# The first sixteen modulation tiles on TensorE, and the first norm in two groups, in a two-layer diffusion trunk

## The reference

```python
mod = silu(cond) @ ada_w[l] + ada_b[l]      # 9 x 1024 numbers, once for c_ctx and once for c
h   = x * rsqrt(mean(x * x) + 1e-6) * g[0] * (1 + scale) + shift
y   = (silu(h @ w_gate) * (h @ w_up)) @ w_down
```

## Time and profile before

| | |
|---|---|
| median of 3 timed runs | 2817.86 us (2813.22 to 2823.29) |
| the profiled execution | 2814.35 us, span 2812.5 us |
| PE busy | 2671.0 us, 95% |
| DVE busy | 1471.0 us, 52% |
| ACT busy | 1040.7 us, 37% |
| DMA | 320.21 MB, mean 114 GB/s |
| mean granted PE clock | 0.97 |

### The profile page before, as it was taken

One profiled execution on the slowest core, in us unless ns is written; L12 is line 12 of the kernel. 1 busy time (PEld: TensorE's weight loads), 2 busy tenths in 40 slices (PEclk: granted clock), 3 DMA queues, 4 the chain that ended last, 5 costly groups with the idle time before them and its releaser, 6 DMA issues.

```text
span 2812.5 us, 41918 instructions
## 1 busy us (share of the span) xinstructions
PE 2671.0 (95%) x17263; PEld 2556.0 (91%) x17263; DVE 1471.0 (52%) x2362; ACT 1040.7 (37%) x1574; POOL 3.7 (0%) x5
## 2 busy tenths in 40 slices
PE   6999999998886999999999999999989989999998
PEld 6999999885676889999999999999878888999998
DVE  6888334533436367763356775336565436322334
ACT  4333343444543353222345322334433345222333
POOL 0000000000000000000000000000000000000000
PEclk7999999999987999999999999999989999999999
DMA  6666234320000145542445553344210013322344
GB/s 237 209 204 207 77 130 149 123 68 24 1 1 23 53 144 186 185 134 95 149 134 181 188 187 112 108 151 142 73 60 1 1 60 106 112 75 75 105 146 140
DMA packets 87771, 320.21 MB, mean 114 GB/s; under 512 B 12486, under 2 KB 16598, under 8 KB 87126
## 3 DMA queue, kind: packets, MB, share of 16 engines
q1 hardware_dynamic: 87638, 318.37, 34.0%
HBM read 312.44 MB, written 3.23 MB: 112 GB/s over the span
## 4 chain that ended last, share of the span: by engine, by line
PE 87%; DVE 7%; ACT 4%; issue 1%; DMA 1%; SPq 1%; DVEq 0%; ACTq 0%
PE ps L2119 41%; PE ps L2148 30%; PE ps L949 2%; PE ps L707 2%; PE ps L2177 2%; PE ps L567 1%; ACT w_hi L402 1%; DVE w_lo L408 1%; PE ps L512 1%; DVE xsq L1924 1%; PE ps L935 1%; PE ps L938 1%; PE ps L937 1%; DVE hx_lo L1933 1%; PE ps L1323 0%
## 5 line engine op out<-in xcount | busy, mean ns | idle before, releaser
L408 DVE TENSOR_TENSOR w_lo<-w_raw,w_hi 128x1024 fp32r<-128x1024 f32 (+1 forms) x384 | 521.3, 1358 | 943.2 <-ACT w_hi L402 942.5
L402 ACT CAST w_hi<-w_raw 128x1024 fp32r<-128x1024 f32 (+1 forms) x384 | 443.9, 1156 | 1227.9 <-PE ps L2119 715.8
L2119 PE MATMUL ps<-hx_hi,w_hi 128*128 128x320 f32 x2688 | 612.5, 309 | 6.9 <-DVE w_lo L408 3.2
L2119 PE MATMUL ps<-hx_lo,w_hi 128*128 128x320 f32 x2688 | 611.6, 308 | 0.0
L2119 PE MATMUL ps<-hx_hi,w_lo 128*128 128x320 f32 x2688 | 611.3, 308 | 0.0
L2119 PEld LDWEIGHTS ps<-hx_hi,w_hi 128*128 128x128 f32 x2688 | 450.7, 188 | 8.0 <-DVE w_lo L408 3.7
L2119 PEld LDWEIGHTS ps<-hx_hi,w_lo 128*128 128x128 f32 x2688 | 451.1, 188 | 0.0
L2119 PEld LDWEIGHTS ps<-hx_lo,w_hi 128*128 128x128 f32 x2688 | 451.0, 188 | 0.0
L2148 PE MATMUL ps<-hh_hi,w_hi 128*128 128x320 f32 x1408 | 435.5, 309 | 3.0 <-DVE hh_lo L2013 3.0
L2148 PE MATMUL ps<-hh_lo,w_hi 128*128 128x320 f32 x1408 | 433.3, 308 | 0.0
L2148 PE MATMUL ps<-hh_hi,w_lo 128*128 128x320 f32 x1408 | 433.3, 308 | 0.0
(11 more groups left out here) (291 smaller groups left out, 2699.1 us busy)
## 6 DMA issues: line engine op xcount, KB each, us to landing
w_raw<-in_ffn_gu SPq DMA_DIRECT2D x212, 512.0 KB, 3.6
w_raw<-in_ffn_dn SPq DMA_DIRECT2D x128, 704.0 KB, 4.0
ring_a<-in_ada_w SPq DMA_DIRECT2D x96, 512.0 KB, 4.6
ada_top<-in_ada_w SPq DMA_DIRECT2D x32, 512.0 KB, 4.6
w_raw<-in_even_in SPq DMA_DIRECT2D x16, 512.0 KB, 3.6
w_raw<-in_odd_in SPq DMA_DIRECT2D x12, 512.0 KB, 4.4
first_a<-in_ada_w SPq DMA_DIRECT2D x8, 512.0 KB, 12.0
w_raw<-in_even_out SPq DMA_DIRECT2D x8, 512.0 KB, 3.7
```

The costliest lines, as they stand in the source:

```text
L402: nc.scalar.copy(w_hi[:, slot, 0:tiles * P], w_raw[:, slot, 0:tiles * P]).then_inc(hi_done, 1)
L408: nc.vector.tensor_tensor(w_lo[:, slot, 0:tiles * P], w_raw[:, slot, 0:tiles * P], w_hi[:, slot, 0:tiles * P], ALU.subtract).then_inc(lo_d ...
L2119: last = nc.tensor.matmul(ps[:, out_bank + h, 0:TH], w, a[:, k, h * TH:(h + 1) * TH], start=(start and w is wh and a is hi), stop=(stop an ...
```

## The change

All sixteen tiles are made by PE, in the order (0, 8), (1, 9), ..., so that shift and scale of a feature tile come together. They are taken from a new layout `ada_first`, and their sums go into banks 6 (feature tiles 0 to 3) and 7 (4 to 7). DVE finishes the mods of four feature tiles at a time, and makes the norm of these four in both halves (all scaled tiles, then all low parts) before the low part of one weight chunk; then the next four. ACT follows in the same order. `cond_b` is loaded last and its silu is made last; DVE waits for it before block 0. ACT loads the table that has both Ln and Exp once, ahead of the squares. SP loads chunk 0 between the two groups of eight tiles and chunk 1 after the second.

```diff
-        first_order = [0, 1, 8, 2, 3, 9, 4, 5, 10, 6, 7, 11, 14, 12, 15, 13]
-        by_pe, by_dve = range(KT, KT + 6), (*range(KT), 14, 15)
+        first_order = [j for k in range(KT) for j in (k, KT + k)]
+        def nth_in(i, h, k):
+            return nth(i, h, k) if i else KT * (k // 4) + 4 * h + k % 4 + 1
...
-            sp.dma_start(cond_col[:], io["cond_col"]).then_inc(col_loaded, 16)
-            load_cond()
+            for dst, name in ((cond_col, "cond_col"), (ada_bias, "ada_b"), (norm_g, "norm_g")):
+                sp.dma_start(dst[:], io[name]).then_inc(col_loaded, 16)
...
-            for q in range(2):
-                load(q, q, ffn_gu[0, 0, q], 8, wait=False)
+            load_first(range(KT))
+            load(0, 0, ffn_gu[0, 0, 0], 8, wait=False)
+            load_first(range(KT, 2 * KT))
+            load(1, 1, ffn_gu[0, 0, 1], 8, wait=False)
+            sp.dma_start(cond_b[:], io["cond"]).then_inc(cond_loaded, 16)
...
-            silu_cond(0)
+            nc.scalar.preload_act_table_set("natural_log_exp_and_others")
...
-                    for q in range(2):
-                        split_hi(act, q, q, 8, wait_used=False)
-                    high(0, 0, every)
-                    high(0, 1, every)
+                    split_hi(act, 0, 0, 8, wait_used=False)
+                    for g in range(2):
+                        for h in range(2):
+                            high(0, h, range(4 * g, 4 * g + 4))
+                    split_hi(act, 1, 1, 8, wait_used=False)
+                    silu_cond(0)
...
-            dve.wait_ge(cond_ready, 1)
-            for i, j in enumerate(by_dve):
-                wait_first(dve, j)
-                ada_column(ada_first(j), j, first_used, i)
-            dve.wait_ge(first_used, len(by_dve))
-            dve.wait_ge(scale_done, len(by_pe))
-            link(dve, dve_chain, nc.vector.tensor_copy(mods[:, KT:KT + len(by_pe), :],
-                                                       ps[:, 7, 0:2 * len(by_pe)].rearrange("p (j c) -> p j c", c=2)))
-            finished(0, 0, 0, 2).then_inc(mods_ready, 1)
-            dve.wait_ge(mods_ready, 1)
-            for q in range(2):
-                split_lo(dve, q, q, 8, wait_used=False)
+            def first_mods(g):
+                dve.wait_ge(scale_done, g + 1)
+                for part in range(2):
+                    cols = slice(KT * part + 4 * g, KT * part + 4 * g + 4)
+                    ins = nc.vector.tensor_tensor(mods[:, cols, :], ps[:, 6 + g, 8 * part:8 * part + 8].rearrange(
+                        "p (j c) -> p j c", c=2), ada_bias[:, cols].unsqueeze(2).broadcast_to((P, 4, 2)), ALU.add)
+                link(dve, dve_chain, ins)
+                for ci in range(2):
+                    ins = nc.vector.scalar_tensor_tensor(out=mods[:, cols, ci], in0=mods[:, cols, ci], scalar=1.0,
+                                                         in1=norm_g[:, 0, 0, 4 * g:4 * g + 4], op0=ALU.add, op1=ALU.mult)
+                ins.then_inc(mods_ready, 1)
+                dve.wait_ge(mods_ready, g + 1)
...
-                    normed(0, 0)
-                    normed(0, 1)
+                    dve.wait_ge(col_loaded, 48)
+                    for g in range(2):
+                        tiles = range(4 * g, 4 * g + 4)
+                        first_mods(g)
+                        for h in range(2):
+                            scaled(0, h, tiles)
+                        for h in range(2):
+                            low(0, h, tiles)
+                        split_lo(dve, g, g, 8, wait_used=False)
+                    dve.wait_ge(cond_ready, 1)
...
             def first_scales():
                 pe.wait_ge(col_ready, 1)
-                for i, j in enumerate(by_pe):
-                    wait_first(pe, j)
-                    for k in range(KT):
-                        ins = nc.tensor.matmul(ps[:, 7, 2 * i:2 * i + 2], ada_first(j)[:, k * P:(k + 1) * P],
-                                               cond_col[:, k, :], start=(k == 0), stop=(k == KT - 1))
+                for g in range(2):
+                    for i in range(KT * g, KT * g + KT):
+                        j = first_order[i]
+                        a = 8 * (j // KT) + 2 * (j % 4)
+                        wait_first(pe, j)
+                        for k in range(KT):
+                            ins = nc.tensor.matmul(ps[:, 6 + g, a:a + 2], ada_first(j)[:, k * P:(k + 1) * P],
+                                                   cond_col[:, k, :], start=(k == 0), stop=(k == KT - 1))
                     ins.then_inc(scale_done, 1)
```

More of the change, by code:

```diff
@@ L310, in build @@
         ada_loaded = [sem(f"ada_loaded{q}") for q in range(ADA_RING)]
-        first_used, ada_used = sem("first_used"), sem("ada_used")
+        ada_used = sem("ada_used")
         silu_done, mul_done, hhi_done, block_free = sem("silu_done"), sem("mul_done"), sem("hhi_done"), sem("block_free")
@@ L1544, in load_ada, with load_first @@
                 sp.dma_start(ada_ring(n), ada_w[ADA_FIRST + n]).then_inc(ada_loaded[n % ADA_RING], 16)
-            sp.dma_start(cond_col[:], io["cond_col"]).then_inc(col_loaded, 16)
-            load_cond()
+            for dst, name in ((cond_col, "cond_col"), (ada_bias, "ada_b"), (norm_g, "norm_g")):
+                sp.dma_start(dst[:], io[name]).then_inc(col_loaded, 16)
             for k in range(KT):
                 sp.dma_start(xT[:, k, :], io["x"][:, k, :]).then_inc(x_loaded, 16)
-            for i, j in enumerate(first_order):
-                src = io["ada_scale"][j - KT] if j in by_pe else ada_w[j]
-                sp.dma_start(ada_first(j), src).then_inc(first_loaded[i // 4], 16)
+            def load_first(tiles):
+                for i in tiles:
+                    j = first_order[i]
+                    sp.dma_start(ada_first(j), io["ada_first"][j]).then_inc(first_loaded[i // 4], 16)
             def load(c, slot, src, tiles, wait=True):
@@ L1650, in silu_cond @@
             def silu_cond(i):
-                act.wait_ge(cond_loaded, 48 * (i + 1))
+                act.wait_ge(cond_loaded, 16 + 48 * i)
                 nc.scalar.activation(cond_b[:], cond_b[:], ACT.Silu).then_inc(cond_ready, 1)
-            act.wait_ge(col_loaded, 16)
+            act.wait_ge(col_loaded, 48)
             nc.scalar.activation(cond_col[:], cond_col[:], ACT.Silu).then_inc(col_ready, 1)
-            silu_cond(0)
+            nc.scalar.preload_act_table_set("natural_log_exp_and_others")
             def rms(bank, h, sums, value, done):
@@ L1679, in high @@
                 for k in tiles:
-                    act.wait_ge(pre_ready, nth(i, h, k))
+                    act.wait_ge(pre_ready, nth_in(i, h, k))
                     for ci, a, b in half_groups(h):
@@ L1773, in _ @@
                             nc.scalar.copy(causal_b[:, :, i, :], causal[:]).then_inc(attn_const, 1)
-                    act.wait_ge(mods_ready, min(s["f"], 2) + 2)
+                    act.wait_ge(mods_ready, min(s["f"], 2) + 3)
                     nc.scalar.preload_act_table_set("natural_log_exp_and_others")
@@ L1930, in low @@
                 for k in tiles:
-                    dve.wait_ge(hxhi_ready, nth(i, h, k))
+                    dve.wait_ge(hxhi_ready, nth_in(i, h, k))
                     for ci, a, b in half_groups(h):
@@ L2037, in _ @@
                                 ins.then_inc(mods_ready, 1)
-                                dve.wait_ge(mods_ready, s["f"] + 2)
+                                dve.wait_ge(mods_ready, s["f"] + 3)
                     else:
@@ L2144, in half_product @@
                     if ready is not None:
-                        pe.wait_ge(hx_ready, ready + t)
+                        pe.wait_ge(hx_ready, ready(t))
                     wh, wl = w_hi[:, q, t * P:(t + 1) * P], w_lo[:, q, t * P:(t + 1) * P]
@@ L2161, in in_products @@
                         half_product(2 * q + h, q, hx_hi, hx_lo, 0, KT, h, True, True,
-                                     ready=None if q else nth(i, h, 0), count=h == 1)
+                                     ready=None if q else lambda t: nth_in(i, h, t), count=h == 1)
             def post_sums(i, h):
@@ L2214, in gu_half @@
                             half_product(4 * par + 2 * q + h, q, hx_hi, hx_lo, 0, KT, h, True, True,
-                                         ready=nth(n, h, 0) if q == 0 and st in (0, lag) else None)
+                                         ready=(lambda t: nth_in(n, h, t)) if q == 0 and st in (0, lag) else None)
                             if st == 0 and q == 0 and after:
@@ L2294, in lay_out @@
     out["cond_col"] = c(np.stack([f["c_ctx"], f["c"][0]]).T.reshape(KT, P, 2).transpose(1, 0, 2))
-    w = f["ada_w"][0][:, D:2 * D].reshape(KT, P, KT, P)
-    out["ada_scale"] = c(w.transpose(2, 1, 0, 3)).reshape(KT, P, D)
+    w = f["ada_w"][0][:, 0:2 * D].reshape(KT, P, 2 * KT, P)
+    out["ada_first"] = c(w.transpose(2, 1, 0, 3)).reshape(2 * KT, P, D)
```

1 line of the change is left out of this document (added).

## The result

The changed kernel takes 2858.0 us (median of 4 runs, 2856.39 to 2861.69), the kernel before beside it 2815.54 (2812.20 to 2823.29). The ratio is 1.014, 95% interval 1.0111 to 1.0169: it is slower, by 42 us, where 0.5 us were forecast, which would not have been measurable. Later series of the same two kernels gave 1.0104 (1.0057 to 1.0152) and 1.013 (1.0098 to 1.0161).

What follows compares the result with a forecast made beforehand. The bound was when PE gets its first full supply of operands, before 57 us, behind DVE's chain. +0.2 for the second quarter and +0.3 for the clock's rise gave +0.5 us: 2814.9 profiled, 2818.4 by the median, range 2811 to 2825.

Steps and rivals of the forecast that it cites:

- Step 2: Before the norm: 20 DVE products (24.8 us) go; PE makes 128 small matmuls instead of 96, ending at 47.3.
- Step 1: Start of the kernel: x loads ahead of cond_b, 2.6 us earlier; sums of squares on PE from 12.4 to 24.0.
- Steps 3 to 5: Norm groups and first products: DVE's first group hidden, then a 3.4 us wait for PE; second quarter at 57.9, +0.2.
- rival A: Clock stays up through the small matmuls; DVE bounds, second quarter at 52.0, 2806.1 to 2808.7 profiled; chance 0.10.
- Step 6: First products on PE: the clock rises at 62.0 to 63.0 instead of 61.8, taken as +0.3 us.
- Step 7: Later waits, for cond_b's late silu before DVE's first block and for chunk 3's later load: cost nothing.
- B: PE doesn't reach full clock before the products, sums of squares at half pitch: 10 later, 2824.8 profiled; chance 0.05.
- C: ACT, not DVE, paces the second norm group; second quarter 1 to 2 us later, 2816 to 2817; chance 0.10.
- D: DVE's relief shows later, in the blocks: worth 0, the same time as the forecast, chance 0.75 together with it.

Runs made afterwards that it cites:

- e1: The changed kernel with three of the eight k in each small product (96 records instead of 256): 2820.55 us, ratio 1.0017 to the kernel before.
- r0: The changed kernel run again with no edit, in rounds beside the kernel before: median 2850.89 us of four runs.
- e3: The changed kernel with one full fp32 product of 320 columns behind each tile's small matmuls: 2860.80 us, ratio 1.0149 to the kernel before.

## Why the prediction was wrong

**Step 2 failed, by a count; it is 28.0 of the 42.6 us.** The prediction set "128 small matmuls where it had 96". The 96 of the trace are records, and an fp32 matmul leaves two of them: the program has six tiles of eight matmuls, 48, for the 96 records of the earlier trace rows, and the 16 matmuls of the sums of squares are the x32 there. (The fp32r products leave one each: the 72 of L2167 in the chain are three quarters of 24.) The change has 16 x 8 = 128 matmuls, so 256 records. The term was one number of the code set beside one number of the trace. With 256, and the prediction's own rates and bounds: 41 until 28.5, then 215 x 0.216 = 46.4, end at 74.9; measured 75.5. The second quarter at 74.9 + 0.1 + 0.7 + 8.5 + 1.2 = 85.4; measured 85.83. That is 27.7 us later, measured 28.15; with its 0.3 for the clock's rise the blocks begin 28.0 later instead of 0.5, measured 28.03. That the last two agree so well is partly luck: the time from the second quarter to the blocks was not 0.3 longer but 0.1 shorter (12.97 us, 13.09 before). All the rest of the step was right: PE as the bound, the fall after 4.5 us (4.3), the two rates, and no limit by the loads.

**Step 1** was right in kind: the sums begin at 13.46 (12.4 predicted, 15.04 before); the squares of x could start 1.6 us earlier, not 2.6. That is 1 us of the sum; the sums themselves took 11.4 instead of 11.6.

**Steps 3 to 5** hold to tenths. Mods 0.54 (0.7), scaled 4.3, low parts 4.2, low part of the chunk 1.15: from the second mods to the second quarter 10.26 us, 10.5 predicted. DVE waited 17 us for the second group instead of 3.4, since PE was 28 us late. In e1, where DVE sets the pace, the second quarter started at 51.11; rival A, the DVE-bound case, had 52.0. (e1's clock fell too, at 28.1; with 96 records even half clock leaves DVE as the bound.)

**Step 6**: the clock was up again at 90.6, 4.8 us after the second quarter's start, within the 4.1 to 5.1 that were used. **Step 7**: nobody waited for the silu of cond_b; it ended at 85.45 and DVE's next work came at 96.46.

**The rivals.** A didn't happen: the clock fell. B didn't either: the sums of squares went from 0.53 us a weight load to the full rate 5.5 us after their start (18.93), as they had before (20.51). The granted clock is shown as 1.00 in the slow part too, so it is the pitch that tells. C didn't: ACT kept up. D holds: DVE's relief showed nowhere; from the blocks to 500 us PE waits once for DVE, 0.8 us, in both kernels. None of them held the case that came, because all took over the same count. The Trainium skill, "TensorE: Matmul & The Clock Gate", section "LDWEIGHTS (loading the stationary operand)", gives one formula for a weight load, its columns divided by 1.2, which is 107 ns for 128 columns. Some 217 records at 0.213 contradict it as a price at any clock. Nor does the trace agree at 2.4 GHz as the prediction said: 0.109 is the pitch of a record, and a matmul has two, so it costs 0.218 there and 0.426 at 1.2 GHz. By the rows, even a clock that stayed up would have needed 28 us for the 128, not rival A's 14.0.

**What the sum left out** is the other 14.4 us. Everything behind the first products was put at nothing, because no instruction there is changed. But the first mixer can take 437.8 or 458.6 us for the same work, and it took 14.4 us more in the profile after. The prediction read the spread of three runs (10 us) and took it for noise around a fixed kernel; the fifteen runs beside r0 span 2803.7 to 2830.9. The profile of before had the shortest mixer of all, so part of the 14.4 is luck of that execution; that the changed kernel's runs are 10 to 14 us long beyond the stage on average isn't, and its cause stays open.

The same error can be seen in the page without any run: two records for one instruction stand in the earlier trace rows (x32 for the 16 squares of 8 tiles and 2 halves).

## What to carry to other kernels

Before a count of the code is multiplied by a duration of the trace, one group is counted in both; fp32 matmuls have two records each here. Work moved from one engine to another is to be priced at the rate that the new engine has after some microseconds of that work alone: here a PE given only matmuls of two columns went to half clock after 3.9 to 4.5 us (4.5 before, 4.3, 3.9 and 4.4 in the three profiles of the changed kernel), and 3.41 us for a tile is worse than the 2.48 that DVE took for it. A stage on the path is compared by its own marks in the profile, and a total only against the scatter of many runs.

## What was not expected of the hardware

PE's clock falls and rises at places of the mixer that differ from execution to execution, and the mixer's length goes with them: 437.8 and 437.9 us in one pair of executions of two different programs, 454.6 and 454.6 in another. The Trainium skill, "TensorE: Matmul & The Clock Gate", section "Part 1: The HAM clock gate (the "warmup" mystery)", has it that what watches the engine's activity isn't restarted with a kernel, so the same kernel can meet it in different phases. The three mixers of the changed kernel (452.2, 458.6 and 454.6 us) and the equal pairs agree with that; no run here shows the phase itself. The page speaks of the first matmuls of a kernel, and puts the penalty of that ramp under 1% of a typical kernel's span. Here the 21 us between the shortest and the longest mixer, 0.7% of the span, arise in the middle of the kernel, and a change of a few us is hidden by them. PE's small matmuls keep the clock down even with a full fp32 product of 320 columns behind every sixteen records (e3: still 3.41 us for the last sixteen).
